# Three expert passes of a hybrid encoder with the token halves side by side, experts put in order by their counts, and attention groups in a new order

## The reference

```python
def swiglu(x, wg, wu, wd):                       # layer 0: 1024 -> 4096 -> 1024
    a = jnp.einsum('bsd,df->bsf', x, wg); b = jnp.einsum('bsd,df->bsf', x, wu)
    return jnp.einsum('bsf,fd->bsd', jax.nn.silu(a) * b, wd)

# layer 1: each token goes to its 2 best experts of 8, each expert 1024 -> 3584 -> 1024
logits = xt @ w_router; top_logit, top_idx = lax.top_k(logits, 2)
gates = softmax(top_logit)
y = (silu(xb @ w_gate[e]) * (xb @ w_up[e])) @ w_down[e]    # xb: the tokens of expert e
out[tokens of e] += y * gate

# attention: token grid 4 x 64; each query sees all 4 rows and 16 columns around it,
# with a relative bias per head, softmax, then the weighted sum of the values
```

## Time and profile before

| | |
|---|---|
| runs | 1568.06, 1568.49, 1570.18 us |
| profiled execution | 1569.15 us; its span 1567.3 us |
| attention, layers 0 and 1 | about 46 to 113 us and 457 to 513 us |
| dense mixer | about 150 to 420 us |
| routing | about 549 to 566 us |
| experts | 566 to 1549 us, one each 122.6 us |
| granted clock, mean of the span | 0.98 |
| loads of one expert | 21 of 2048.0 KB, 44.0 MB |

### The profile page before, as it was taken

One profiled execution on the slowest core, in us unless ns is written; L12 is line 12 of the kernel. 1 busy time (PEld: TensorE's weight loads), 2 busy tenths in 40 slices (PEclk: granted clock), 3 DMA queues, 4 the chain that ended last, 5 costly groups with the idle time before them and its releaser, 6 DMA issues.

```text
span 1567.3 us, 20797 instructions
## 1 busy us (share of the span) xinstructions
PE 1499.1 (96%) x8037; PEld 1116.4 (71%) x8037; DVE 1185.6 (76%) x926; ACT 954.6 (61%) x846; POOL 151.0 (10%) x194
## 2 busy tenths in 40 slices
PE   5898999999899889999999999999999999999996
PEld 5787999999799656666666666666666666666663
DVE  4566544444657578898898899889889889889886
ACT  4345434444444457777777677677777777777674
POOL 3221300000001269500000000000000000000000
PEclk9898999999999989999999999999999999999998
DMA  9617654555530548999999999999999999999992
GB/s 287 199 57 225 203 208 168 185 191 178 211 129 30 199 151 314 356 367 351 355 370 349 358 365 351 357 363 360 350 368 356 359 361 356 367 373 367 350 356 81
DMA packets 182051, 442.01 MB, mean 282 GB/s; under 512 B 4057, under 2 KB 6113, under 8 KB 182001
## 3 DMA queue, kind: packets, MB, share of 16 engines
q1 hardware_dynamic: 179856, 433.42, 75.7%
q0 software_dynamic: 2144, 7.90, 1.8%
HBM read 440.26 MB, written 1.05 MB: 282 GB/s over the span
## 4 chain that ended last, share of the span: by engine, by line
PE 92%; DVE 3%; DMA 2%; SPq 1%; ACT 1%; issue 1%; POOL 0%; DVEq 0%; ACTq 0%
PE pc L589 17%; PE pc L590 16%; PE pc L591 16%; PE pd L589 9%; PE pd L590 9%; PE pd L591 9%; DMA rwords_b<-in_na_rpb 2%; PE pd L669 2%; PE pa L589 1%; PE pa L591 1%; PE pa L590 1%; PE pb L591 1%; PE pb L590 1%; PE pb L589 1%; PE pb L836 1%; PE pb L653 1%
## 5 line engine op out<-in xcount | busy, mean ns | idle before, releaser
L1362 DVE TENSOR_TENSOR w_lo<-ring,w_hi 128x2048 fp32r<-128x2048 f32 x288 | 658.5, 2289 | 96.0 <-ACT w_hi L1048 95.0
L1048 ACT ACTIVATE w_hi<-ring 128x2048 fp32r<-128x2048 f32 x288 | 550.7, 1915 | 119.2 <-PE pc L591 75.6
L589 PE MATMUL pc<-w_hi,xT_hi 128*80 128x512 f32 x896 | 355.9, 397 | 1.8 <-DVE xT_lo L1379 1.8
L590 PE MATMUL pc<-w_lo,xT_hi 128*80 128x512 f32 x896 | 352.7, 394 | 0.0
L591 PE MATMUL pc<-w_hi,xT_lo 128*80 128x512 f32 x896 | 350.4, 391 | 0.0
L1156 DVE TENSOR_TENSOR w_lo<-ring,w_hi 128x2048 fp32r<-128x2048 f32 x72 | 167.1, 2322 | 143.3 <-ACT w_hi L918 143.0
L591 PEld LDWEIGHTS pc<-w_hi,xT_lo 128*80 128x80 f32 x896 | 132.8, 148 | 74.7 <-issue 0.5
L589 PEld LDWEIGHTS pc<-w_hi,xT_hi 128*80 128x80 f32 x896 | 132.8, 148 | 70.9 <-issue 2.3
L918 ACT ACTIVATE w_hi<-ring 128x2048 fp32r<-128x2048 f32 x72 | 137.2, 1907 | 71.8 <-PE pb L591 55.7
L590 PEld LDWEIGHTS pc<-w_lo,xT_hi 128*80 128x80 f32 x896 | 133.1, 149 | 66.9 <-issue 0.4
L589 PE MATMUL pd<-w_hi,eT_hi 128*80 128x512 f32 x448 | 176.3, 393 | 0.0
(11 more groups left out here) (254 smaller groups left out, 1945.7 us busy)
## 6 DMA issues: line engine op xcount, KB each, us to landing
ring<-in_moe_w_gate SPq DMA_DIRECT2D x48, 2048.0 KB, 8.0
ring<-in_moe_w_up SPq DMA_DIRECT2D x48, 2048.0 KB, 9.6
ring<-in_moe_w_down SPq DMA_DIRECT2D x48, 2048.0 KB, 12.2
ring<-in_dense_w_gate SPq DMA_DIRECT2D x8, 2048.0 KB, 8.5
ring<-in_dense_w_up SPq DMA_DIRECT2D x8, 2048.0 KB, 8.6
ring<-in_dense_w_down SPq DMA_DIRECT2D x8, 2048.0 KB, 7.7
spare<-in_moe_w_down SPq DMA_DIRECT2D x8, 2048.0 KB, 13.4
spare<-in_moe_w_up SPq DMA_DIRECT2D x8, 2048.0 KB, 12.7
```

Source lines behind the costliest of these rows:

```text
L589: mm(dst, still[0], moving[0], start=start, stop=False)
L590: mm(dst, still[0], moving[1], start=False, stop=False)
L1048: act.activation(hi, src, ACT.Copy).then_inc(hi_ready, 1)
L1362: dve.tensor_tensor(lo, src, hi.bitcast(F32), ALU.subtract).then_inc(split_ready, 1)
```

## The change

- Room per expert is CAP = 128 tokens for five passes and PAIR = 64 for three. Pass 0 is expert 0. Passes 1, 3, 5 take the three with the fewest tokens of the others, passes 2, 4, 6, 7 the rest; GpSimd ranks the counts in `plan_items`, and SyncE reads the expert's number before it issues the loads of passes 1 to 7.
- A pass of 64 (`paired_pass`) holds the high parts of 64 tokens and their low parts in one 128 x 128 tile. Each weight tile meets it in two matmuls: the high weights stream against all 128 columns, the low weights against the 64 high columns (`both`). The low tokens' sums come out in partitions 64 to 127. ScalarE copies them to `low`, and TensorE adds them to partitions 0 to 63 by a product with a shifted identity (`fold`). A tiny product with zeros closes the sum of the upper partitions. The order is `PAIRED`: gate b, up b, down b-1.
- The passes of 128 turn and split full 128-wide tiles (`ident`, `x2`, `e2`) in place of 80-wide ones.
- In the attention a group is now two rho by two m, issued so that neighbouring matmuls of `scores` use different 32-partition slices and PSUM banks. `values` handles two groups at once, with the four rho innermost; it is called after `fill` at g = 4, 5 and 7 and at the end. The bias is stored in the new order.

The diff at its core:

```diff
+def paired_order(blocks):
+    order = []
+    for b in range(blocks):
+        order += [("gate", b), ("up", b)]
+        if 0 < b < blocks - 2:
+            order.append(("down", b - 1))
+    return order + [("down", b) for b in range(blocks - 3, blocks)]
...
             sp.wait_ge(scored, GROUPS * DEPTH)
-            with sp.Fori(0, NE) as e:
-                load_item(e, e)
+            load_item(0, 0, EXPERT)
+            sp.wait_ge(order_ready, 1)
+            with sp.Fori(0, PAIRS) as k:
+                expert = sp.value_load(order[0:1, bass.ds(k * 2 + 1, 1)], min_val=0, max_val=NE - 1)
+                load_item(k * 2 + 1, expert, PAIRED)
+                expert = sp.value_load(order[0:1, bass.ds(k * 2 + 2, 1)], min_val=0, max_val=NE - 1)
+                load_item(k * 2 + 2, expert, EXPERT)
...
                 pool.wait_ge(slots_ready, 1)
+                link(pool.tensor_scalar(key, cnt, float(NE), None, ALU.mult))
+                link(pool.tensor_tensor(key, key, key_off, ALU.add))
+                compare(big, by_expert(key), key.unsqueeze(2).broadcast_to([P, NE, NE]), ALU.is_gt)
+                sum_last(rank.unsqueeze(2), big, NE)
+                compare(perm, by_expert(rank), item_rank.unsqueeze(2).broadcast_to([P, NE, NE]), ALU.is_equal)
+                link(pool.tensor_tensor(big, perm, by_expert(numbers), ALU.mult))
+                sum_last(item_expert.unsqueeze(2), big, NE)
+                pool.tensor_copy(order[0:1, :], item_expert[0:1, :]).then_inc(order_ready, 1)
+                for src, mine, dst in ((pos, item_slot, item_pos), (gates, item_gates, item_gate)):
+                    link(pool.tensor_tensor(moved, ..., ALU.mult))
+                    sum_last(te(mine).unsqueeze(3), moved, NE)
+                    pool.tensor_copy(dst[:, :, 1:NE], te(mine)[:, :, 1:NE]).then_inc(items_ready, 1)
...
-                    for m in range(4):
-                        q = qT[rows32, m, b * P:(b + 1) * P]
-                        ...
-                        ins = mm(pa[:, m * 256:m * 256 + ROWS * WIN], q, k, start=True, stop=True)
+                    for mi in range(2):
+                        for ri in range(2):
+                            m, rho = 2 * mp + mi, 2 * rp + ri
+                            rows32 = slice(HD * rho, HD * (rho + 1))
+                            ...
+                            at = ri * C4 + mi * C2
+                            ins = mm(pa[:, at:at + ROWS * WIN], q, k, start=True, stop=True)
...
-                def values(g):
+                def values(pair):
+                    b, mp = pair // 2, pair % 2
+                    ...
+                    for mi in range(2):
+                        m = 2 * mp + mi
                         for kt in range(2):
+                            for rho in range(4):
+                                c = (4 * m + rho) * HD
+                                probs = pt((2 * pair + rho // 2) % 4)[:, kt, 2 * (rho % 2) + mi, :]
+                                ins = mm(pd[HD * rho:HD * (rho + 1), b * C4 + m * P:b * C4 + (m + 1) * P],
+                                         vv[:, kt, c:c + HD], probs, start=kt == 0, stop=kt == 1)
...
+            def paired_pass(i, k):
+                def both(dst, still, moving, start, stop):
+                    if start:
+                        mm(dst, still, moving[0], start=True, stop=False)
+                        return mm(dst[0:PAIR], still[:, 0:PAIR], moving[1], start=False, stop=False)
+                    mm(dst[0:PAIR], still[:, 0:PAIR], moving[1], start=False, stop=False)
+                    return mm(dst, still, moving[0], start=False, stop=stop)
+
+                def fold(at, low_ready, folded, b):
+                    pe.wait_ge(low_ready, k * EBLOCKS + b + 1)
+                    mm(pc[0:PAIR, at:at + C4], shift[:, :], low[:, :], start=False, stop=True).then_inc(folded, 1)
+                ...
+                            for d in range(4):
+                                dt = 4 * c + d
+                                ins = both(pc[:, at:at + C4], x2[:, 0, dt, :], [w[:, d, :] for w in parts],
+                                           dt == 0, False)
+                            if c == 1:
+                                ins = mm(pc[PAIR:P, at:at + 2], ident[:, 0:PAIR], zeros, start=False, stop=True)
...
                             if b == 0:
-                                make_picks(i + 1)
+                                dve.wait_ge(items_ready, 2)
+                                make_picks(i + 1, cap)
```

More of the change, by code:

```diff
@@ L544, in plan_items @@
                 link(pool.tensor_scalar(row[:, 0:7], row[:, 0:7], float(NE - 1), None, ALU.min))
+                for n in range(EXTRA):
+                    compare(tmp8, numbers, row[:, n:n + 1].broadcast_to([P, NE]), ALU.is_equal)
+                    link(pool.tensor_tensor(tmp8, tmp8, item_expert, ALU.mult))
+                    sum_last(row[:, n:n + 1], tmp8, NE)
                 link(pool.tensor_copy(row[:, 7:8], inc[:, 7:8]))
@@ L1369, in make_picks, with tokens_gathered @@
                 for t in range(NT):
[L1370 removed]
+                    for first in range(0, P, cap):
+                        ins = dve.tensor_scalar(pick[:, t, first:first + cap], iota[:, 0:cap], cur[:, 0, t:t + 1], None,
+                                                ALU.is_equal)
                 ins.then_inc(pick_ready, 1)
[L1373 removed]
+            def tokens_gathered(i, cap):
@@ L1384, in combined, with results_out @@
+            def results_out(i):
+                dve.wait_ge(half_done, i * PH + MH + PH)
+                for j in range(2):
+                    part = slice(j * C4, (j + 1) * C4)
+                    dve.wait_ge(ynat_hi_ready, i * 2 + j + 1)
+                    dve.tensor_tensor(ynat_lo[:, part], pd[:, part], ynat_hi[:, part].bitcast(F32),
+                                      ALU.subtract).then_inc(ynat_ready, 1)
             def combined(i, t):
@@ L1390, in combined, with splits @@
                     dve.tensor_tensor(q, q, pa[:, j * C4:(j + 1) * C4], ALU.add).then_inc(facc_done, 1)
-            def expert_pass(i, first, last):
+            def splits(i, first, last):
                 ahead = [first]
@@ new lines, in expert_pass, with paired_pass, finish @@
+                results_out(i)
+                split_until(PH + 3)
+            def paired_pass(i, n):
+                split_until = splits(i, 3, PH + 3)
+                def finish(b):
+                    dve.wait_ge(up_folded, n * EBLOCKS + b + 1)
+                    dve.wait_ge(esilu_ready, i * EBLOCKS + b + 1)
+                    if b == 0:
+                        dve.wait_ge(spread_ready, i + 1)
+                    hidden_product(PAIR)
+                    if b == 0:
+                        make_picks(i + 1, CAP)
+                for j, (what, b) in enumerate(PAIRED):
+                    for c in range(2):
+                        k = 2 * j + c
+                        if what == "gate" and b and c == 1:
+                            finish(b - 1)
+                        if (what, b, c) == ("down", EBLOCKS - 3, 1):
+                            finish(EBLOCKS - 1)
+                        if what == "up" and b == 0:
+                            combined(i, c)
+                        split_until(k + 3)
+                        if what == "up" and b and c == 0:
+                            hidden_turned(i, b - 1, PAIR)
+                        if (what, b, c) == ("gate", 4, 0):
+                            tokens_gathered(i + 1, CAP)
+                        if (what, b, c) == ("down", EBLOCKS - 2, 0):
+                            hidden_turned(i, EBLOCKS - 1, PAIR)
+                            tokens_in(i + 1, CAP)
+                results_out(i)
```

412 lines of the change are left out of this document (264 added, 148 removed).

## The result

The changed kernel takes 1544.6 us (median of four runs, 1543.0 to 1553.8) against 1568.8 for the kernel before on the same chip: a ratio of 0.986 (95% interval 0.982 to 0.990). It is faster, by about 24 us (1.4%), where I had forecast 55 us slower. The profiled execution took 1545.4 us, 23.7 less than the one before.

The account below looks back on a forecast made before the run. TensorE's instruction stream was taken to bound the expert passes at 122.6 us, VectorE 14 us below. 1569.15 - 16.2 (attention) + 10.0 (wide passes) + 62.1 (passes of 64) = 1625.1, median 1624 us; range 1536 to 1648.

Parts of the forecast that it names:

- Part 1: Attention's new order: value products and scores run side by side on array slices, 16.2 us less over two layers.
- Rival C: Attention gains nothing, with the switch cost paid: 1640 us; no chance of its own, counted in the forecast's 0.67.
- Part 2: Five wide passes: 128-wide transposes cost 1.6 us more a pass, with switches and start +10.0 us, bounds 0 and 15.
- Part 3: Three passes of 64: fewer matmuls but paid shape changes, 143.3 us a pass against 122.6, +62.1 us in all.
- What a change of the array's shape costs: Passes of 64: 0.19 us into the full shape, 0.14 into the narrow, 23 each way a block, 53.1 us a pass.
- The bound of 0: Passes of 64: lower bound of nothing paid per shape change, as 80-wide matmuls switch for free beside 128-wide ones.
- my 90.2: TensorE's time in us for a pass of 64 without the price of shape changes.
- Rival A: Passes of 64: a 64-wide matmul changes no shape, 114 us a pass, 1537 us in all; chance 0.20.
- Some waits between them: Passes of 64 without shape costs: VectorE about 108 us and DMA 110, taken with waits as 114 a pass.
- The stated range: Whole kernel: 1536 to 1648 us, taking in rival B (0.12) and the upper part of Rival A's neighbourhood.
- my own range: Whole kernel: the main forecast's own range, 1610 to 1645 us, chance 0.67.
- Part 4: Items costed at nothing: GpSimd's ranking with 11 us of cover, the expert-number read, buffer filling and covered waits.

Follow-up runs that it names:

- experiment 10: The changed kernel with each expert load issued as two halves of 1024 KB, each once its part is split: 1533.3 us, ratio 0.978 to the kernel before.
- experiment 4: The changed kernel with passes 1, 3 and 5 run as wide passes of three products and 128 tokens: 1562.5 us, ratio 0.996 to the kernel before.

## Why the prediction was wrong

- **Part 1, the attention: right.** -16.2 forecast; with the attention alone 13.5 us less by the medians, and the mark of pass 0 17.2 us earlier by the one trace. 32 value products cost 1.0 us where I took 1.6, since four slices side by side cost 0.03 each and not 0.045; scores 0.77 as forecast (0.8). Rival C falls.
- **Part 2, the wide passes: too dear.** +10.0 forecast. A wide pass between wide ones takes 1.0 us more, not 1.6; the three ahead of a paired pass take 122.5, no more than before (with all passes wide they take 123.6). At the start +1.5 for 1.0, by the marks of two traces that scatter by more. In all about +1.
- **Part 3, the failed step.** "What a change of the array's shape costs", 53.1 us a pass: between the full and the narrow products it is 0, and only the zero products pay 0.09 each. So the three passes, forecast at +62.1 us, measured -7.6. I read the price from the earlier trace rows, where the small side is in plain float32, and in rows 6 small in rows and not in columns, and carried it to a product of few columns in the one-pass format. In bfloat16 the price is near the forecast (0.31 for 0.33 a pair, 41 us for 53.1 a pass); in the one-pass format fewer rows do pay (0.43 against 0.23), fewer columns don't. The bound of 0 stood in the forecast, with the reason that proved right (80-wide and 128-wide mix freely in this same format); I went by the wrong neighbour, the one near in width and not the one alike in format. Without that term TensorE's stream is 97 us (measured with both halves taken away), 7 more than my 90.2; where the 7 lie is open.
- **Rival A, right in kind, too hopeful in size.** 114 us a pass forecast, 117.3 to 122.6 measured. "Some waits between them" were worth 10 to 15 us over VectorE's 107, not 6: two bounds within some 4 us of each other (44.0 MB at 398 GB/s are 111), coupled through four buffers, and a jump. The stated range, 1536 to 1648, holds 1544.6 only because it was drawn down to this rival, which had 0.20; my own range began at 1610.
- **Part 4: right** for the ranking (11.3 us of cover). What I had costed at nothing without naming it, the jump of a loop with a wide and a paired pass in it, costs TensorE 2 us at the end of passes 1 and 3, and 5 a pass, with the slower clock behind it, once the loads come in halves and hide less.

## What to carry to other kernels

Take the price of a change of shape from a row in the same number format as the instruction that you cost; nearness in width says less. Look also at where the weight load starts: where it ran one matmul ahead nothing was paid, where it started with its own matmul 0.1 to 0.2 us. When an engine stops being the bound, the next bounds are not worth their own busy time: here 107 and 111 us made 117 to 123, and loads handed over in halves and loops written out gave most of the difference back. A finer hand-over is worth nothing while TensorE is the bound.

## What the runs showed of the hardware

- Narrow columns beside full ones: one-pass float32 0.23 us a matmul either way; bfloat16 0.33 against 0.22, with the weight load starting only at its own matmul. Fewer rows cost in the one-pass format too: 0.43 against 0.23.
- Slices of the columns used in turn run side by side in full: two of 64 take 3.6 us for 32 matmuls in bfloat16 where full ones take 7.0; four of 32 in plain float32 1.8 us, where 64 columns alone take 7.0.
- The loads ran at 398 to 399 GB/s over whole passes (113 to 116 us) when the splits took half as long.
- A loop with about 1000 matmuls in it costs TensorE 2 to 4 us at its jump back. After 3.6 and 4.0 us of idle time (experiment 10) the granted clock is at the lower level for about 3.4 us; after the changed kernel's two waits, 2.2 and 2.0 us, it stays at 1.00 once and falls once. The kernel before, with one pass in its loop, shows no such wait, and with two wide passes in the loop (experiment 4) it is 0.2 and 0.8 us. That it hangs on the jump is shown by the loops written out; what in the jump takes the time, and why it differs so, is open. One sign: between 700 and 1400 us the instruction queues of the profile moved nothing in the kernel before, 41 packets in the changed kernel and 34 in experiment 4, as if the code of one pass stayed and that of two were brought in anew. That alone is not the wait, for the loops written out move 38 packets and don't wait.
